# Six modulations of a second layer, moved from the end of a recurrent loop into the routing of a mixture of experts

## The reference, cut to what matters

```python
for l in range(DEPTH):                       # DEPTH = 2
    mod_lat = (silu_c @ ada_w[l] + ada_b[l])[:, None, :]
    mod_ctx = (silu_cc @ ada_w[l] + ada_b[l])[None, None, :]
    sh1, sc1, g1, sh2, sc2, g2 = jnp.split(mod_lat, 6, axis=-1)
    ...
    h_lat = modulate(x_lat, norm_mix_g[l], sh1, sc1)
    o_lat, o_ctx = even_mixer(...)           # layer 0: attention heads and mLSTM heads, then @ w_out
    x_lat = x_lat + g1 * o_lat
    h_lat = modulate(x_lat, norm_ffn_g[l], sh2, sc2)
    y = moe(...)                             # routing, then 16 experts, SwiGLU
    x_lat = x_lat + g2 * y_lat
```

## Time and profile before

| | |
|---|---|
| median of 3 runs | 1796.3 us (1795.85 to 1797.65) |
| the profiled execution | 1792.2 us, its span 1790.6 us |
| mean granted clock of TensorE | 0.927 |
| PE busy | 1568.0 us (88%) |
| DVE, ACT, POOL busy | 550.9, 340.3, 86.8 us |
| DMA | 371.18 MB, mean 207 GB/s |
| chain that ended last | PE 70%, DMA 16%, DVE 8%, ACT 3% |

### The profile page before, as it was taken

How to read it: one execution, slowest core, us unless ns; L and a number is a source line. 1 busy time by engine, 2 the same in 40 slices (tenths; PEclk the granted TensorE clock), 3 DMA queues, 4 the chain that set the end, 5 groups by cost and what they waited for, 6 DMA issues and landing times.

```text
span 1790.6 us, 27476 instructions
## 1 busy us (share of the span) xinstructions
PE 1568.0 (88%) x11350; PEld 1110.4 (62%) x11350; DVE 550.9 (31%) x1368; ACT 340.3 (19%) x744; POOL 86.8 (5%) x135
## 2 busy tenths in 40 slices
PE   7999889999869999999795899999669988777783
PEld 5787578885624756655442899988545665444442
DVE  2602722306354237305714111111056623001011
ACT  1311401113131123114304000000141312000001
POOL 0001000001100000000100200000100001000000
PEclk9899888998979999998898999999879998999987
DMA  7358423466624244220541799999752025999996
GB/s 250 100 168 262 152 75 85 146 200 220 159 76 137 71 134 151 94 71 1 187 148 49 289 392 396 399 393 401 279 186 95 24 95 191 392 390 399 395 404 239
DMA packets 183595, 371.18 MB, mean 207 GB/s; under 512 B 19412, under 2 KB 138032, under 8 KB 167008
## 3 DMA queue, kind: packets, MB, share of 16 engines
q1 hardware_dynamic: 164352, 322.90, 50.6%
q0 software_dynamic: 10560, 32.73, 5.8%
q10 hardware_dynamic: 8608, 14.51, 2.3%
HBM read 345.52 MB, written 24.59 MB: 207 GB/s over the span
## 4 chain that ended last, share of the span: by engine, by line
PE 70%; DMA 16%; DVE 8%; ACT 3%; issue 2%; SPq 0%; ACTq 0%; POOL 0%; POOLq 0%; DVEq 0%
PE ps_proj L575 29%; DMA ring<-in_exp_w 14%; PE ps_outp L575 13%; PE ps_proj L1178 6%; PE ps_outp L1178 4%; PE ps_score L1178 4%; PE ps_score L575 4%; PE ps_proj L701 2%; PE ps_turn L728 2%; DVE probs L1827 1%; DVE rstd L1806 1%; PE ps_turn L575 1%; PE ps_proj L633 1%; DVE h_t L2023 1%; PE ps_score L797 1%
## 5 line engine op out<-in xcount | busy, mean ns | idle before, releaser
L575 PE MATMUL ps_proj<-h_t,ring 128*128 128x256 f32 (+1 forms) x1280 | 360.9, 443 | 16.4 <-ACT h_t L1523 8.1
L575 PEld LDWEIGHTS ps_proj<-h_t,ring 128*128 128x128 f32 x1280 | 252.5, 199 | 122.6 <-issue 86.4
L1178 PE MATMUL ps_proj<-ring,arena 128*32 128x128 f32 (+2 forms) x2048 | 155.9, 388 | 37.4 <-DMA ring<-in_exp_w 35.1
L1178 PEld LDWEIGHTS ps_proj<-ring,arena 128*32 128x32 f32 (+1 forms) x2048 | 122.4, 118 | 68.4 <-DMA ring<-in_exp_w 48.6
L1178 PE MATMUL ps_score<-ring,arena 128*32 128x384 f32 (+2 forms) x2048 | 152.1, 386 | 13.7 <-DMA ring<-in_exp_w 13.7
L1178 PE MATMUL ps_outp<-ring,arena 128*32 128x384 f32 (+3 forms) x1792 | 148.7, 412 | 9.1 <-DMA ring<-in_exp_w 7.2
L1178 PEld LDWEIGHTS ps_score<-ring,arena 128*32 128x32 f32 (+1 forms) x2048 | 118.5, 118 | 42.9 <-DMA ring<-in_exp_w 23.1
L1178 PEld LDWEIGHTS ps_outp<-ring,arena 128*32 128x32 f32 (+1 forms) x1792 | 100.7, 117 | 45.7 <-DMA ring<-in_exp_w 13.8
L2269 DVE COPY arena<-ps_score 128x384 f32<-128x384 f32 (+1 forms) x32 | 15.7, 491 | 318.9 <-PE ps_score L1207 318.9
L575 PE MATMUL ps_proj<-ring,h_t 128*128 128x256 f32 (+1 forms) x512 | 106.4, 366 | 0.4 <-ACT arena L1547 0.4
L1376 ACT ACTIVATE arena<-ps_proj 128x512 f32<-128x512 f32 (+1 forms) x70 | 40.1, 576 | 330.6 <-PE ps_proj L575 328.5
(11 more groups left out here) (284 smaller groups left out, 1582.9 us busy)
## 6 DMA issues: line engine op xcount, KB each, us to landing
ring<-in_exp_w SPq DMA_DIRECT2D x192, 1024.0 KB, 11.4
ring<-in_ada_w SPq DMA_DIRECT2D x48, 1024.0 KB, 6.2
ring<-in_w_in SPq DMA_DIRECT2D x30, 1024.0 KB, 5.8
ring<-in_even_w_in SPq DMA_DIRECT2D x12, 1024.0 KB, 5.6
ring<-in_w_out SPq DMA_DIRECT2D x8, 1024.0 KB, 6.5
expert_in<-arena POOLq DMA_DIRECT2D x1, 6144.0 KB, 27.6
ring<-in_odd_w_in SPq DMA_DIRECT2D x6, 1024.0 KB, 11.6
arena<-expert_in POOLq DMA_DIRECT2D x15, 384.0 KB, 8.1
```

Of the source, the lines that this page charges most:

```text
L575: last = pe.matmul(out, w, a, start=(i == 0), stop=(i == len(pairs) - 1))
L1178: last = pe.matmul(b[p0:p0 + pn, c0:c0 + wn], x_of(p0, lo, pn), w[:, w0:w0 + wn], start=first and p0 not in strip[:i], stop=done and p0 no ...
```

## The change

The six modulations leave steps 6 to 11 of the mLSTM loop. Two of them stand ahead of the router's matmul and four behind the transposes of the tokens, ahead of the wait for the choice. On ScalarE the two are emptied behind the shift and the table load for the sigmoid, ahead of the logits; the four behind the last tokens. Their weights stand behind those of the output projection in the stream. The sum, transpose, bias and gains go behind the expert loop. POOL's written order is as it was: its last six `modulation_rows` and `modulation_back(1)` stand ahead of the scatter, and now carry out their work in the routing.

```diff
--- before.py
+++ after.py
@@ -467,9 +467,9 @@
         modulation_weights(1, 0, 12)
         for c in range(1, 6):
             add(((0, KC, 256), k_cols(ew, 1536 + 256 * c, 256)))
-        modulation_weights(1, 12, 24)
         for c in range(4):
             add(((0, KC, 256), k_cols(dr["even_w_out_2"][0], 256 * c, 256)))
+        modulation_weights(1, 12, 24)
         MOE = ["moe", "moe"]
 
 
@@ -501,7 +501,6 @@
 
         FIRST = EXPERTS * CAP[0]
         STEPS = 2 * HEADS
-        BESIDE = range(STEPS - 2, STEPS + 4)
         moe = {}
 
 
@@ -1069,8 +1068,6 @@
                     mark["hturn", h] = use["turn"]
                 if h >= 1 and i % 2 == 0:
                     head_sums("ones", head_sq)
-                if i in BESIDE:
-                    modulation()
             pe.wait_ge(head_ready, 12)
 
             def slot_out(w):
@@ -1086,6 +1083,9 @@
                 t0 = T2 - n
                 h = h_t[:, 0:KC * n].rearrange("p (c t) -> p c t", c=KC)
                 ready = mixer_input()
+                if l == 0:
+                    modulation()
+                    modulation()
                 b = claim("proj")
                 for k in range(KC):
                     q = 32 * (k % 4)
@@ -1109,7 +1109,8 @@
                         mark["router", l] = use["proj"]
                 mark["h_tok", l] = use["proj"]
                 if l == 0:
-                    modulation_turned(1)
+                    for _ in range(4):
+                        modulation()
                 else:
                     for t in range(NB):
                         for c in range(0, KC, 4):
@@ -1284,6 +1285,8 @@
                     with pe.Fori(1, more) as i:
                         tile(i)
 
+                if l == 0:
+                    modulation_turned(1)
                 for t in range(n // P if l == 0 else 0):
                     pe.wait_ge(mixed, 4 * l + t + 1)
                     for c in range(0, KC, 4):
@@ -1614,8 +1617,6 @@
                 h = i // 2 - 1
                 if h >= 1 and i % 2 == 1:
                     head_root(8 + h - 1, P)
-                if i - 1 in BESIDE:
-                    modulation_out()
                 if i + 1 < STEPS:
                     if (i + 1) % 2 == 0:
                         products((i + 1) // 2)
@@ -1632,6 +1632,9 @@
                 rms_root(n)
                 shift(h, l, 1, n)
                 warm_up(ACT.Sigmoid)
+                if l == 0:
+                    modulation_out()
+                    modulation_out()
                 evac(logit_t[:, 0:n], n=n)
                 for t in range(n // P):
                     for c in range(0, KC, 4):
@@ -2164,8 +2170,6 @@
                 nb = n // P
                 h = h_t[:, 0:KC * n].rearrange("p (c t) -> p c t", c=KC)
                 normalise(h, n)
-                if l == 0:
-                    modulation_sum(1)
                 dve.wait_ge(drained["proj"], mark["router", l])
                 sc, se, pk, wk = (t[:, 0:nb, :] for t in (score, sel, pick, work))
                 g4 = lambda t: t.rearrange("p b (g e) -> p (b g) e", g=4)
@@ -2247,9 +2251,6 @@
                 dve.tensor_tensor(part[:, :, 0:nb], part[:, :, 0:nb], tq.unsqueeze(1).to_broadcast([P, 2, nb]), ALU.mult
                                   ).then_inc(part_ready, 1)
                 dve.wait_ge(part_ready, l + 1)
-                if l == 0:
-                    modulation(1)
-
                 def rows_in(e):
 
                     for q in range(2):
@@ -2298,6 +2299,10 @@
                         dve.wait_ge(of_pe[l], 3 + 4 * i)
                         dve.tensor_copy(act_t.rearrange("p c t -> p (c t)"), bank["score"][1][:, :]
                                         ).then_inc(of_dve[l], 1)
+
+                if l == 0:
+                    modulation_sum(1)
+                    modulation(1)
 
                 def mix(t):
```

## The result

The changed kernel takes 1813.63 us, the median of 4 runs (1811.7 to 1814.65), against 1796.97 us of the kernel before on the same chip (4 runs, 1795.85 to 1800.21): a ratio of 1.0091, interval 1.0074 to 1.0107, so 16.7 us slower. Forecast were 1807.3 us, 1800.5 to 1815, slower with 0.87. Run once more in a later session as e11, it gave 1.0087 (1.0070 to 1.0103).

What follows compares the result with a forecast made beforehand. In the experts PE and DMA are both full, PE setting the pace by a hair. Expert 1's late rows give +13.0 us, the earlier projection -2.0: 1796.3 + 11.0 = 1807.3 us, range 1800.5 to 1815.

Steps and rivals of the forecast that it cites:

- the sum's highest case: Whole kernel: VectorE 14 us late, scatter delayed 6.3, rows' load 8.1; +19 us.
- Part 1: Tail of the mLSTM loop: projection starts 2.94 us earlier, 0.9 lost to low clock; -2.0 us (-2.9 to -1.6).
- Part 2: Two modulations ahead of the router: they hold both banks until ScalarE empties them; routing 4.4 us late (2.8 to 4.7).
- Part 3: Four modulations ahead of the wait for the choice: the last waits for weights; VectorE resumes 11.9 us later.
- Part 4: Sums behind the expert loop: PE's gather no longer waits for them, so starts only 6.1 us later; far end costs nothing.
- Part 5: POOL's scatter and expert 1's rows: load issued 11.9 us later plus 2.5 scatter delay, taking 6.5; rows land at 1023.7.
- The sum: End of expert 1's score: 1037.0 instead of 1024.0, +13.0 us; with the projection's earlier start +11.0, 1807.3 us.
- Its own signs: Trace: projection about 892, score matmul near 989, first scatter about 10 us later, PE waiting for banks, weights and rows.
- The scatter at its old pace: Trace of POOL's scatter: keeping its old pace beside weights would show the prediction wrong.
- crowded queue: Scatter shares the DMA equally with weights, expert 1's rows land 6 us later than summed: +17, 1813 us; chance 0.17.
- Light queue: Routing: weights land at their shortest, scatter hardly disturbed: +2.5 to +6, 1799 to 1802 us; chance 0.17.
- Faster, as the change reads: Six modulations stand in pauses and block nothing, VectorE not late: -4.8, 1791.5 us; chance 0.06.

Runs made afterwards that it cites:

- e11: The changed kernel itself, run once more in a later session beside the others: 1.0087, 1814.19 us.
- e4: The changed kernel with two of the six modulations left in the mLSTM loop at steps 6 and 7, two behind the transposes: 1.0041, 1804.22 us.
- e1: The changed kernel with ScalarE emptying the first two modulations' banks between the halves of the shift: 1.0072, 1811.42 us.
- e5: The kernel before with only the modulation's sum, transpose, bias and gains moved behind the expert loop: 0.9992, 1796.22 us.
- e7: The changed kernel with SyncE waiting for expert 1's rows before requesting expert 1's weights: 1.0073, 1808.4 us.
- e3: As e2, with POOL's last two modulation stores and the load back moved behind the load of expert 1's rows: 1.0136, 1821.11 us.
- e10: As e3, with SyncE holding expert 1's weights until expert 1's rows have landed: 1.0115, 1817.29 us.
- e8: Kernel before, four modulations in the loop, two ahead of the router, banks emptied between shift halves, late sums, expert 1's weights held for rows: 0.9995, 1797.45 us.
- e6: As e5, with SyncE waiting for expert 1's rows before requesting expert 1's weights: 0.9992, 1798.37 us.
- e2: The changed kernel with PE's four later modulations moved behind the matmul of the counts: 1.0097, 1815.19 us.
- e9: Kernel before, four modulations in the loop, two ahead of the router, banks emptied between shift halves, sum behind row_ready, transpose behind counts: 0.9996, 1798.59 us.

## Why the prediction was right, and what was off

Sign and range held: slower, and 1813.6 lies between 1800.5 and 1815. The range held by 1.4 us, and with some luck: less the 2.0 us of upstream the two traces lie 19.8 us apart, more than the +19 of the sum's highest case. The mechanism is the one forecast, but for the scatter, which no weights slowed down: banks blocked ahead of the router, late weights for the last modulation, late counts, late rows, PE idle ahead of expert 1, the same 17.4 us an expert from there on. The forecast is 6.3 us low, and the terms show where. Parts 2 to 5 are counted from the norm on, which is 2.16 us late in the trace (the 2.0 of upstream and the 0.2 of part 1):

- **Part 1, forecast -2.0, measured +0.2.** The step that failed is the cost of the clock: it counted only the first microseconds of the projection (0.9, measured 0.7). The modulations had also kept PE at 2.4 GHz inside the loop, where VectorE waits for PE. e4 shows that as 1.5 us; the two matmuls of the norm's sums, which took 1.94 us for 1.12, are the rest.
- **Part 2, forecast 4.4.** The logits are emptied at 977.13 instead of 970.63: +6.5, less the 2.16, 4.3. Right, and e1 confirms the cause.
- **Part 3, forecast 11.9, measured 15.1** (17.25 less 2.16). The last weights were taken to land 7.0 us after their request, 3.0 behind the first. They landed 8.70 us after it (+1.7), 4.2 behind the first; the loads of expert 0 had been requested from 986.64 on, and that these shared the DMA is the likely reason. Behind that wait the last half modulation took 1.93 us at the low clock where 0.97 was counted (+1.0). And the third modulation began 0.6 us later than summed, since the first transposes behind the router took 1.88 us for 1.45. Together 3.3, for the 3.2 of the difference.
- **Part 4, forecast +6.1 for the gather, measured 9.9.** The 5.8 us of the moved bias were gained (e5 shows 5.7); 15.1 - 5.8 = 9.3, and 0.6 came from the counts at the low clock (1.12 us for 0.67) and the steps behind them. Not in the sum at all is gate 0 at 8.9 us for 5.2, which here lies beside the wait for the rows. The far end costs nothing, as said.
- **Part 5.** The rows' load was to be issued 14.4 late and was issued 15.8 late (1020.78 against 1002.82, less 2.16). Of the 14.4, 2.5 were for a scatter slowed by weights, and that was zero: POOL reached it so late that the weights had nearly passed. The load itself took 9.08, not 6.5, since it went out behind expert 1's weights (e7). Then came the turn and gate 1 at the low clock, +2.7, which the sum had at full clock; the same step as part 1, a wait that costs more than its length.
- **The sum:** 13.0 forecast, + 1.4 (issue) + 2.6 (load) + 2.7 (clock) = 19.7 at the end of score 1, and with the 2.16 21.9, where the trace has 1045.87 - 1024.0 = 21.9. The medians make 16.7. Of the 5 us between, 2.0 are those of upstream; the other 3 are not placed. The profiled execution of before lies 4.8 us under its median. The stretch behind score 1 takes 765.7 to 773.8 us in the 13 traces (766.6 before), with the same work in all of them but for the place of the sums, so chance has room there too. And in the trace of before the rows' load won its race by 1.3 us; whether the longer executions lose that race no trace shows.
- **Its own signs.** The waits named as signs are all there, the times later than named: net of upstream the projection at 893.5 for about 892, the counts at 994.4 for near 989, POOL's first scatter 16 us later for about 10. The scatter at its old pace was named as a sign of being wrong if it came beside weights; it came, but the weights had nearly passed.

The rival *crowded queue* has the nearest number, 1813, by another way: in the changed kernel the scatter wasn't slowed. e3 and e10 show that its mechanism exists, at a larger price than it was given, as soon as the scatter is early enough to meet the weights. *Light queue* is out by the 8.70 and 9.08 us. *Faster, as the change reads* named its own condition, counts by 979.13 + 2.8 and banks emptied within the shift. e8 meets both, with the sums late and the projection 2.9 us earlier, though only two of its six stand in a pause, and gains nothing; so its price seems wrong too. The rows, the expert's weights and the clock then bound PE at nearly the same place, within 3 us.

## What to carry to other kernels

A pause of an engine is free for other work only if the result buffers and the weights of that work are free of it too: count the banks it holds, which instruction of which engine empties them, and what its freed slots request. When two transfers of unequal size become due at nearly the same time, it matters which is requested first; but to hold the large one back for the small one moved the wait to the large one here, and gave nothing (e6) or 3 to 4 us that the times alone don't show clearly (e7, e10). An early scatter into a full DMA may land later than a late one. And filler work beside a chain of small steps may be worth its place for the clock alone.

## What the runs showed of the hardware that was not expected

- **The clock inside a sparse chain.** The same 20 weighted-value records take 4.71 us at 1.2 GHz in one run of matmuls, or 0.91 + 1.83 us, 0.43 us of wait between, with one modulation beside each step (e4 against the changed kernel). After waits of 3.2 to 13.4 us ahead of gate 1 (for rows or for weights), it took 6.8 to 8.2 us instead of 5.45.
- **A scatter against loads.** Issued into a queue of weights it took 17.6 us (e10) and 22.3 us (e3) from the end of its last issue, against 3.7 to 5.3 us in the others; its 4.2 MB got 131 of some 415 GB/s over all of e3, but 2.77 MB against 3.01 over 1004 to 1018.
- **A small load behind large ones.** 384 KB: 3.7 to 4.9 us ahead of expert 1's weights (before, e6, e7, e8, e10), 9.1 to 10.0 us within 1 us behind the first of them (the changed kernel, e1, e4, e5, e11), 8.2 us in e2, some 2 us behind, and 6.6 us in e3, some 12 us behind.
- **Gaps in gate 0.** In the nine traces in which gate 0 runs while POOL issues the scatter, the matmuls come, behind the first 42 to 61 records, in bursts of mostly 4 or 5 every 1.43 us. The gate takes 8.9 to 11.2 us for 5.2. Nothing that the profile shows ends the gaps, and they stop 1.3 to 1.6 us behind the last issue (1015.91 and 1017.26 in the changed kernel; 997.25 and 998.77 in e5). In the four in which gate 0 starts behind it (before, e3, e9, e10) it takes 5.45 us, in e3 and e10 beside a full DMA, so a full DMA alone does not make them. What links the two is not settled; no run separates POOL's issues from the scatter's traffic.
